# Inverse norms and forget decays spread by split float32r matmuls, scores and values alternating halves of the array

## The reference, cut to what matters

```python
def forgetting_attention(q, k, v, f_logit, g_q, g_k):
    q = rms(q) * g_q                      # norm over the 64 channels of each head
    k = rms(k) * g_k
    dcum = cumsum(log_sigmoid(f_logit), axis=1)
    logits = q @ k.T * scale + dcum[query] - dcum[key]
    p = softmax(where(k_pos <= q_pos, logits, MASK_VALUE))
    return p @ v
```

## Time and profile before

| | |
|---|---|
| median of 3 executions | 2930.14 us |
| lowest, highest | 2928.32, 2937.82 us |
| profiled execution, its own time | 2927.02 us |
| its span in the profile | 2925.2 us |
| TensorE busy | 2671.4 us, 91% of the span |
| VectorE busy | 1849.8 us, 63% |
| ScalarE busy | 1531.7 us, 52% |
| mean granted TensorE clock | 0.942 |
| SwiGLU and experts | about 264 to 508 and 815 to 1795 us of the span |
| squared-ReLU feed-forwards | about 2175 to 2359 and 2728 to 2911 us |

### The profile page before, as it was taken

One profiled execution on the slowest core, in us unless ns is written; L12 is line 12 of the kernel. 1 busy time (PEld: TensorE's weight loads), 2 busy tenths in 40 slices (PEclk: granted clock), 3 DMA queues, 4 the chain that ended last, 5 costly groups with the idle time before them and its releaser, 6 DMA issues.

```text
span 2925.2 us, 38625 instructions
## 1 busy us (share of the span) xinstructions
PE 2671.4 (91%) x16826; PEld 2361.0 (81%) x16826; DVE 1849.8 (63%) x1553; ACT 1531.7 (52%) x1468; POOL 0.2 (0%) x4
## 2 busy tenths in 40 slices
PE   6978999897899999999999997988799999788998
PEld 6758999775778778787787876877689988768998
DVE  4455444445488888888888886555465555546554
ACT  4423334432377767776777765555444444644443
POOL 0000000000000000000000000000000000000000
PEclk9778999876899999999999999999899999889999
DMA  6103455220189999999898986322145543222452
GB/s 228 68 34 114 175 188 187 101 85 17 46 341 364 348 351 367 348 359 352 350 366 349 368 349 242 130 101 102 68 148 189 186 145 128 74 101 101 159 180 94
DMA packets 83100, 585.33 MB, mean 200 GB/s; under 512 B 9480, under 2 KB 11208, under 8 KB 12272
## 3 DMA queue, kind: packets, MB, share of 16 engines
q1 hardware_dynamic: 82928, 582.81, 53.3%
HBM read 581.73 MB, written 1.05 MB: 199 GB/s over the span
## 4 chain that ended last, share of the span: by engine, by line
PE 82%; DVE 11%; ACT 6%; issue 1%; DMA 0%; ACTq 0%; SPq 0%; DVEq 0%
PE PS L1325 80%; ACT whi L492 2%; DVE wlo L824 2%; ACT pb L551 1%; DVE stat L912 1%; PE PS L1661 1%; DVE pb L920 1%; ACT pt L567 1%; DVE aT L1007 1%; DVE hT L1002 1%; DVE hT L841 1%; PE PS L1457 1%; DVE small L837 1%; DVE hT L885 0%; DVE qe L1028 0%
## 5 line engine op out<-in xcount | busy, mean ns | idle before, releaser
L824 DVE TENSOR_TENSOR wlo<-raw,whi 128x2048 fp32r<-128x2048 f32 x550 | 1259.7, 2292 | 591.7 <-ACT whi L492 581.3
L492 ACT ACTIVATE whi<-raw 128x2048 fp32r<-128x2048 f32 x550 | 1052.3, 1914 | 372.3 <-PE PS L1325 366.5
L1325 PE MATMUL PS<-hhi,whi 128*128 128x256 f32 x1952 | 572.3, 293 | 35.3 <-DVE hlo L847 33.5
L1325 PE MATMUL PS<-hlo,whi 128*128 128x256 f32 x1952 | 564.1, 289 | 0.0
L1325 PE MATMUL PS<-hhi,wlo 128*128 128x256 f32 x1952 | 563.5, 289 | 0.0
L1325 PEld LDWEIGHTS PS<-hhi,whi 128*128 128x128 f32 x1952 | 386.1, 198 | 51.6 <-issue 48.9
L1325 PEld LDWEIGHTS PS<-hlo,whi 128*128 128x128 f32 x1952 | 387.2, 198 | 0.1
L1325 PEld LDWEIGHTS PS<-hhi,wlo 128*128 128x128 f32 x1952 | 386.6, 198 | 0.0
L1325 PE MATMUL PS<-whi,xghi 128*128 128x512 f32 x896 | 360.2, 402 | 2.1 <-ACT pm L648 2.1
L1325 PE MATMUL PS<-whi,xglo 128*128 128x512 f32 x896 | 354.8, 396 | 0.0
L1325 PE MATMUL PS<-wlo,xghi 128*128 128x512 f32 x896 | 354.8, 396 | 0.0
(11 more groups left out here) (317 smaller groups left out, 3793.9 us busy)
## 6 DMA issues: line engine op xcount, KB each, us to landing
raw<-in_wm SPq DMA_DIRECT2D x336, 1024.0 KB, 4.9
raw<-in_ws SPq DMA_DIRECT2D x214, 1024.0 KB, 4.8
xT<-in_xT SPq DMA_DIRECT2D x1, 1024.0 KB, 4.7
bsum<-in_bsum SPq DMA_DIRECT2D x1, 1024.0 KB
out_T<-hT SPq DMA_DIRECT2D x4, 256.0 KB, 2.5
lmask<-in_lmask SPq DMA_DIRECT2D x1, 512.0 KB
tri<-in_tri SPq DMA_DIRECT2D x1, 256.0 KB
cmask<-in_cmask SPq DMA_DIRECT2D x1, 256.0 KB
```

What stands on the lines that cost most here:

```text
L492: act.activation(whi[s % SPLIT][:], raw[s % RAW][:], ACT.Copy).then_inc(hi_ready, 1)
L824: dve.tensor_tensor(wlo[s % SPLIT][:], raw[s % RAW][:], whi[s % SPLIT][:].bitcast(F32), ALU.subtract).then_inc(lo_ready, 1)
L1325: return pe.matmul(out, a, b, start=start, stop=stop, skip_group_check=True)
```

## The change

The selectors selT, selCT and onehot become float32r: they are loaded into other tiles and VectorE copies them once, the first two before the first mixer, selCT before the second block. TensorE waits for the copies (`selectors_cast`): for the first before the forget logits of layer 0, for selCT before `second_mixer(0)`. In `head_norm` VectorE rounds the reciprocal into rs_hi and subtracts it to get rs_lo, and TensorE adds two float32r products per tile. Forget decays are split alike: ScalarE writes nd_hi, VectorE nd_lo, and VectorE's wait for both copies stands in front of head_norm now. In forget attention the four score products come first, then eight decay products. Score products go in the order 0, 2, 1, 3, and value products alternate between the two halves of partitions.

```diff
-        selT = base.put("selT", [16, DK, P])
+        selT = base.put("selT", [16, DK, P], F32R)
         rs = base.put("rs", [16, S])
+        rs_hi = at("rs_hi", [16, S], base.top, F32R)
+        rs_lo = at("rs_lo", [16, S], base.top + 4 * S, F32R)
         small = base.put("small", [P, 512])
...
-        onehot = c1.put("onehot", [NH, NH, P])
+        onehot = c1.put("onehot", [NH, NH, P], F32R)
...
-        nd = ra.put("nd", [NH, S])
+        nd_hi = ra.put("nd_hi", [NH, S], F32R)
+        nd_lo = ra.put("nd_lo", [NH, S], F32R)
...
-                act.activation(nd[:], PS[0:NH, 7, 0:S], ACT.Copy, scale=-1.0).then_inc(decay_taken, 1)
+                act.activation(nd_hi[:], PS[0:NH, 7, 0:S], ACT.Copy, scale=-1.0).then_inc(decay_taken, 1)
...
             def head_norm(dst, nt, rows_, gain, banks4):
                 fill()
                 after(hn_rooted)
-                dve.reciprocal(rs[0:rows_, :], rs[0:rows_, :]).then_inc(hn_inverse, 1)
+                step(dve.reciprocal(rs[0:rows_, :], rs[0:rows_, :]))
+                step(dve.tensor_copy(rs_hi[0:rows_, :], rs[0:rows_, :]))
+                dve.tensor_tensor(rs_lo[0:rows_, :], rs[0:rows_, :], rs_hi[0:rows_, :].bitcast(F32),
+                                  ALU.subtract).then_inc(hn_inverse, 1)
                 fill()
...
+                after(decay_taken, 2)
+                dve.scalar_tensor_tensor(out=nd_lo[:], in0=PS[0:NH, 7, 0:S], scalar=-1.0, in1=nd_hi[:].bitcast(F32),
+                                         op0=ALU.mult, op1=ALU.subtract).then_inc(decay_rest, 1)
                 head_norm(qkT, 8, 16, lambda t: qs1[:] if t < 4 else vec1(l, "kg"), [4, 5])
-                after(decay_taken, 2)
                 attention(fox_heads(l), pb1)
...
             after(small_loaded, 16 * 12)
+            dve.tensor_copy(selT[:], selT_in[:])
+            dve.tensor_copy(onehot[:], onehot_in[:]).then_inc(selectors_cast, 1)
             first_mixer(0)
...
                 norm(4 + 2 * l)
                 if l == 0:
                     after(tables_loaded, 16 * len(TABLES2))
+                    dve.tensor_copy(selCT[:], tables["selCT"][:]).then_inc(selectors_cast, 1)
                 second_mixer(l)
...
                     for t in range(t0, min(t0 + 2, nt)):
-                        ins = mm(PS[:, b, (t - t0) * S:(t - t0 + 1) * S], selT_of(t), rs[0:rows_, :], True, True)
+                        out = PS[:, b, (t - t0) * S:(t - t0 + 1) * S]
+                        mm(out, selT_of(t), rs_hi[0:rows_, :], True, False)
+                        ins = mm(out, selT_of(t), rs_lo[0:rows_, :], False, True)
...
-                        for i in range(4):
-                            out = sp[:, i // 2, i % 2, 0:w]
-                            ins = mm(out, *j.pair(i), True, j.decay is None)
-                            if j.decay:
-                                ins = mm(out, *j.decay(i), False, True)
+                        for i in (0, 2, 1, 3):
+                            ins = mm(sp[:, i // 2, i % 2, 0:w], *j.pair(i), i % 2 == 0, j.decay is None)
+                        if j.decay:
+                            for i in range(4):
+                                out = sp[:, i // 2, i % 2, 0:w]
+                                mm(out, *j.decay(i, nd_hi), False, False)
+                                ins = mm(out, *j.decay(i, nd_lo), False, True)
...
-                        for i in range(4):
-                            lo, col = j.place(i)
+                        low, high = (sorted((i for i in range(4) if j.place(i)[0] == lo), key=lambda i: j.place(i)[1])
+                                     for lo in (0, HD))
+                        for two in zip(low, high):
                             for b in range(j.keys // P):
-                                ins = mm(PS[lo:lo + HD, 6, col * P:(col + 1) * P], j.value(i, b), pt[:, i, b, :],
-                                         b == 0, b == j.keys // P - 1)
+                                for i in two:
+                                    lo, col = j.place(i)
+                                    ins = mm(PS[lo:lo + HD, 6, col * P:(col + 1) * P], j.value(i, b), pt[:, i, b, :],
+                                             b == 0, b == j.keys // P - 1)
...
-                empty(6, 2, decay_taken)
-                decay_taken_now = C.now(decay_taken)
+                empty(7, 1, decay_rest)
                 head_norm(8, lambda t: selw[:, t, :], lambda t: selT[:, t, :], 16, hT, [4, 5])
-                pe.wait_ge(decay_taken, decay_taken_now)
+                pe.wait_ge(decay_rest, C.now(decay_rest))
...
             for l in range(DEPTH):
                 norm(4 + 2 * l)
                 if l == 0:
                     after(tables_loaded, 16 * len(TABLES2))
+                    after(selectors_cast)
                 second_mixer(l)
```

23 lines of the change are left out of this document (15 added, 8 removed).

## The result

| kernel | median, us | lowest, highest | granted clock |
|---|---|---|---|
| before | 2930.14 | 2927.66, 2937.82 | 0.942 (profiled) |
| changed | 2912.82 | 2903.02, 2915.15 | 0.936 to 0.942 |

The ratio is 0.9928, 95% interval 0.9914 to 0.9943: 21 us faster (17 to 25), where 2897 was forecast and the range ended at 2909; the two medians alone differ by 17.3. The profiled execution took 2913.32 us (span 2911.6, mean granted clock 0.936). The sign was right; the 30.8 us of the sum were half again as much as the 21 measured. Two executions of the experiments further down, one of only_order (4668.68 us) and one of before beside it (5197.36 us), ran far slower than all others; the ratios leave them out, and the medians, which have them in, would be at most 0.3 us lower without them.

A forecast was written before the change was run, and what follows sets the result against it. TensorE was taken to bound the kernel, with 82% of the last-ending chain. First block 26.0, second block 9.3, selCT cast -4.5: 30.8 us off 2927.0 gives 2896.2, stated as 2897; range 2883 to 2909.

The forecast's parts named there:

- Prices: TensorE: a float32r instruction of 256 columns takes 0.12 us, so a split product costs 0.24 against float32's 0.46.
- Rivals C and D: C: weight loads don't overlap, 2913 us, chance 0.05. D: float32r on 8 and 16 rows costs 0.43, 2953, chance 0.03.
- Forget attention: First block, per layer: jobs 0 and 1 gain 2.6 and 1.6 us, jobs 2 and 3 5.3, limited by VectorE and ScalarE.
- rival B: Denser score products spare TensorE low-clock stretches, so units behind forget jobs run faster: 39.4 us gained, 2888; chance 0.12.
- nd_lo: VectorE's extra operation for the decays' low part delays TensorE's first unit in head_norm: -0.4 us per first-block layer.
- Norms: First block, per layer: split spread products gain 0.85 us net for q and k, 2.15 for yT.
- The cast of selCT: TensorE waits uncovered for VectorE's selCT copy at the start of the second block, once: -4.5 us.
- Value products: Alternating halves shortens 16 products from 1.55 to 1.12 us; 0.9 per first-block layer, 2.6 per second-block layer.
- The second block's norms: Split spread products in qa, y and cc gain 0.74, 0.9 and 0.45 us, 2.1 per layer.
- Rival A: Other engines take more: a slowed unit per first-block layer, second-block values hidden; 20.4 us gained, 2907; chance 0.22.
- signs of being wrong: 16-row products 0.2 us or more apart, second block starting without a gap, or untouched stages (experts, feed-forward) changing in length.
- four faster cases: Forecast (2888 to 2902) 0.55, other engines take more 0.22, clock gains 0.12, weight loads don't overlap 0.05; stated as 0.93.

The follow-up runs named there:

- only_order: Kernel before with one edit: in forget jobs the four scores go first, then the decays, still float32 and unsplit; 2909.99 us, ratio 0.9924.
- only_fox: Kernel before with the forget-attention part alone (scores first, decays split into nd_hi and nd_lo), norms and value order old; 2909.96 us, ratio 0.9917.
- only_values: Kernel before with the new order of the value products and nothing else; 2930.40 us, ratio 0.9998.
- old_values: Changed kernel with the old loop over the value products; 2908.99 us, ratio 0.9924 to before.
- only_norms: Kernel before with the split inverse norms alone (rs_hi, rs_lo, casts of selT and selCT with TensorE's waits); 2929.17 us, ratio 0.9991.
- before_conv: Kernel before with VectorE's short convolution moved behind the last filler unit, nothing else; 2933.25 us, ratio 1.0002.
- after_again: The changed kernel once more, unaltered, five more rounds beside before; 2910.77 us, ratio 0.9934.

## Why the prediction was right and wrong

*Prices.* Right. Split products start 0.12 us apart on 8, 16 and 128 rows, 0.21 at the low clock. Rivals C and D fell with that. The Trainium skill's rule (TensorE: Matmul & The Clock Gate, Part 3, The mechanism) that weight loads overlap products only in another row group is contradicted here again, by rs_hi and rs_lo products, each with its own weight load on the same 16 rows.

*Forget attention.* The mechanism was right, down to the new wait for pt (22.5 us against 22.8) and VectorE's late step 2. The size was low: 18.2 with nd_lo and without values, where the medians of only_fox and before differ by 22.5. In the trace the first block of only_fox gained 20.1 (its offset goes from +0.8 to -19.3); the trace of before, on which the sum was built, is a fast execution, which may be part of the rest. The units behind jobs 1 and 2 did come back to the full clock, 1.5 and 1.0 us per layer, as in rival B. But they gained nothing: from the end of scores(1) to values(1) the stretch shrank from 27.9 to 22.5 us, about the 5.1 to 5.3 that VectorE's and ScalarE's path leaves in the sum, and what the units saved became wait for pt. The prediction also credited the split with what only_order gets by order.

*nd_lo.* Right: 0.41 us, TensorE's unit 0.45 later.

*Norms.* First block right: -0.76 for the low part, then gains of 1.9 and 2.7 us, net of 1.1 and 2.0 per layer (0.85 and 2.15 in the sum).

*The cast of selCT.* Right in the trace, 4.9 (4.5).

*Value products: the step that failed.* "Value products count where TensorE is on the chain", with 2.6 per second-block layer and 0.9 per first-block layer, 7.0 in all. The products shrank as priced (1.55 to 1.1, 2.86 to 1.98), and nothing arrived: only_values measures 0.0002 of the time. Two things ate the gain. A shorter step at the full clock only makes the next wait for pt longer, and such waits were there before the change. In the trace of before:

```profile
1960.46 2.85 PE L1325 MATMUL PS<-pt,vb 128*64 128x128 f32 x16 [5.59 <-ACT pt L567]
```

And work behind a shorter step ran longer at the low clock: in only_values 1.5 us for the unit behind a step that had been priced at double gain, and 1.3 us for the HGRN products of a first-block layer. What fixes the moment at which the clock rises is not shown, as old_values has the same late rise with the old order. The kernel-wide mark is the granted clock, 0.935 against 0.941, though not all of that difference lies behind value steps.

*The second block's norms: failed too.* 4.2 expected, a loss of 0.7 in only_norms' trace, where an untouched second block loses 1.0 in before_conv. Each shortening there is real at its place (0.6, 0.8 and 0.6 us); that it is lost because VectorE and ScalarE have the next step and TensorE then runs slower fits the traces, but no run isolates it. Rival A came nearest: it gave 2907, and the medians are 2911 and 2913. Of its two ingredients the hidden values were right. The other, a unit slowed by 2.6 us per layer behind the wait for pt, was not: values and unit together take 8.2 us there, and took 7.9 before. That its number came close is partly luck, as it also kept the 4.2 us of the norms, which did not come, and had forget attention too low.

*Sum.* Forecast: forget attention 18.2, first block's norms 6.0, second block's norms 4.2, values 7.0, the cast -4.5, together 30.9. By the runs and their traces: 22.5, 5.4, -0.7, 1.0 and -4.9, together 23.3; the whole change measured 17 to 25. The first and the fourth of these are differences of medians, the others of traces, and each may be off by a microsecond or two, so the agreement is no proof. One of the prediction's signs of being wrong came in, small: between the marks at 747.71 and 1806.15, where no step of it lies, the changed kernel takes 0.7 us longer. And its four faster cases have chances that add up to 0.94, not 0.93.

What stays open is what sets these losses in the second block. The profiled execution of the changed kernel lost 4.6 us in that block's second layer; after_again, the same kernel, lost 4.4 in the first and gained 0.8 in the second. only_fox, whose second block is untouched, lost 4.2 from the norm ahead of it to its first feed-forward's norm, while only_order, with the same work there, lost 0.3. The stretches that differ are at the low clock in one and not in the other. In the changed kernel's trace 2.9 us are lost in one group of products that the change doesn't touch, and 2.4 in the last projections; small gains elsewhere bring this to 4.6. The group in the changed kernel and before:

```profile
2598.04 6.58 PE L1341 MATMUL PS<-qc,rotC 96*96 96x256 f32 x16 [2.87 <-ACT vc L751]
...
2615.87 3.69 PE L1325 MATMUL PS<-qc,rotC 96*96 96x256 f32 x16 [2.87 <-ACT vc L743]
```

No run fixed where such stretches fall.

## What to carry to other kernels

Before splitting a product into cheaper passes, look at what stands between its neighbours: here putting like products together, with the halves in turn, took 22 us off, and the split of the decays nothing more. A saving counted on one engine must be followed to the next wait for another; where TensorE meets such a wait soon, a shorter burst only makes a longer idle time, and part of the saving may be paid back at the lower clock. Two edits that each do nothing can lose together, so measure them together as well as apart. When a change makes one engine early, look at once for what in the other's queue could step aside: moving the convolution was worth nothing before the change and some 11 us after it.

## What the runs showed of the hardware

- The mean granted clock can be steady in one program and not in another: 0.934 to 0.936 in eleven executions of only_values, 0.942 in five of old_values, 0.941 or 0.942 in most of before, but 0.936 to 0.942 in the first five of the changed kernel, whose spans went with it (2911.6 us at 0.936, 2901.2 at 0.942).
- Behind an idle TensorE the clock can rise later when less work comes first: 2.86 us of products and then a unit of 6.0 in before, 1.98 and then 7.5 in only_values. It is no rule by itself, as 2.86 and then 7.3 occurs in old_values.
- Between products of different shape some 0.1 to 0.2 us go: a pair of identity products costs 0.61 and not 0.43, and the first nd_hi behind the scores takes 0.23 us to its successor where the others take 0.12 (the first rs_hi behind an idle TensorE takes 0.22 as well, 96.98 to 97.20). The Trainium skill (TensorEngine Tiling (Array Packing), Key Properties) says that a change of mode drains the engine; these rows agree.
- Float32r products of 256 columns cost on 8 and 16 rows what they cost on 128, 0.12 us from start to start at the full clock.
